# Third block of a three-block layer chain: rates and token tiles in one stage, rates on 128 rows, the last two levels of the chunk inverse on their own blocks, constant products between the first steps

## What is computed

```python
def gated_delta_rule(q, k, v, beta, g):
    q = l2_norm(q) * (dk ** -0.5); k = l2_norm(k)
...
    gc = jnp.cumsum(g, axis=-1)
    decay = jnp.exp(jnp.where(tril, gc[..., :, None] - gc[..., None, :], NEG_INF))
    kb = k * beta[..., None]; vb = v * beta[..., None]
    lmat = jnp.where(strict, jnp.einsum('bhncd,bhnsd->bhncs', kb, k) * decay, 0.0)
    rhs = jnp.concatenate([vb, kb * jnp.exp(gc)[..., None]], axis=-1)
    sol = lax.linalg.triangular_solve(lmat + eye, rhs, left_side=True, lower=True, unit_diagonal=True)
    value, k_cumdecay = sol[..., :dv], sol[..., dv:]
    attn_intra = jnp.einsum('bhncd,bhnsd->bhncs', q, k) * decay
    q_dec = q * jnp.exp(gc)[..., None]
    k_tail = k * jnp.exp(gc[..., -1:] - gc)[..., None]
    chunk_decay = jnp.exp(gc[..., -1])
...
```

## Time and profile before

| | |
|---|---|
| median of 3 runs | 2967.48 us (2950.17 to 2970.95) |
| profiled execution | 2967.56 us, span 2966.3 us |
| instructions | 42485 |
| PE busy | 2829.5 us, 95% of the span |
| PEld / DVE / ACT / POOL busy | 2379.1 / 1608.9 / 1058.5 / 614.5 us |
| mean granted clock of TensorE | 0.963 |
| DMA | 210.62 MB, mean 71 GB/s |

### The profile page before, as it was taken

One profiled execution on the slowest core, in us unless ns is written; L12 is line 12 of the kernel. 1 busy time (PEld: TensorE's weight loads), 2 busy tenths in 40 slices (PEclk: granted clock), 3 DMA queues, 4 the chain that ended last, 5 costly groups with the idle time before them and its releaser, 6 DMA issues. The chain is left out here.

```text
span 2966.3 us, 42485 instructions
## 1 busy us (share of the span) xinstructions
PE 2829.5 (95%) x16610; PEld 2379.1 (80%) x16610; DVE 1608.9 (54%) x2432; ACT 1058.5 (36%) x1793; POOL 614.5 (21%) x494
## 2 busy tenths in 40 slices
PE   8989999999999999998999999999898998999998
PEld 6768877778888766856788888976788898999986
DVE  5854556465553464944533336965344455576643
ACT  4362333432222323353423224545344233422223
POOL 2530101121100121441100003355355000111101
PEclk9987899999999999989999999998799999999999
DMA  4200132122223321302222222210000122222221
GB/s 155 94 1 7 65 107 71 36 87 94 97 93 99 111 67 56 100 15 78 88 98 93 92 94 78 86 44 1 6 2 1 44 86 72 86 93 93 92 94 64
DMA packets 60307, 210.62 MB, mean 71 GB/s; under 512 B 7926, under 2 KB 8566, under 8 KB 59990
## 3 DMA queue, kind: packets, MB, share of 16 engines
q1 hardware_dynamic: 58934, 207.39, 21.1%
q10 hardware_dynamic: 1184, 0.59, 0.1%
HBM read 205.84 MB, written 2.10 MB: 70 GB/s over the span
## 5 line engine op out<-in xcount | busy, mean ns | idle before, releaser
L272 PE MATMUL ps<-normed_hi,slab_hi 128*128 128x264 f32 (+2 forms) x2568 | 869.6, 339 | 27.5 <-DVE normed_lo L576 13.1
L274 PE MATMUL ps<-normed_hi,slab_lo 128*128 128x264 f32 (+2 forms) x2568 | 853.5, 332 | 0.0
L273 PE MATMUL ps<-normed_lo,slab_hi 128*128 128x264 f32 (+2 forms) x2568 | 852.1, 332 | 0.0
L153 ACT ACTIVATE slab_hi<-ring 128x1024 fp32r<-128x1024 f32 x376 | 397.2, 1057 | 967.0 <-PE ps L274 954.6
L157 DVE TENSOR_TENSOR slab_lo<-ring,slab_hi 128x1024 fp32r<-128x1024 f32 x360 | 481.3, 1339 | 384.8 <-ACT slab_hi L153 384.4
L272 PEld LDWEIGHTS ps<-normed_hi,slab_hi 128*128 128x128 f32 x2568 | 487.2, 190 | 95.8 <-issue 34.9
L273 PEld LDWEIGHTS ps<-normed_lo,slab_hi 128*128 128x128 f32 x2568 | 487.5, 190 | 52.1 <-issue 4.3
L274 PEld LDWEIGHTS ps<-normed_hi,slab_lo 128*128 128x128 f32 x2568 | 485.7, 189 | 48.9
L272 PE MATMUL ps<-hidden_hi,slab_hi 128*128 128x512 f32 x560 | 220.7, 394 | 5.6 <-DVE hidden_lo L223 5.6
L274 PE MATMUL ps<-hidden_hi,slab_lo 128*128 128x512 f32 x560 | 223.2, 399 | 0.0
L273 PE MATMUL ps<-hidden_lo,slab_hi 128*128 128x512 f32 x560 | 221.3, 395 | 0.0
(11 more groups left out here) (573 smaller groups left out, 4040.3 us busy)
## 6 DMA issues: line engine op xcount, KB each, us to landing
ring<-in_stream SPq DMA_DIRECT2D x376, 512.0 KB, 3.3
h<-in_x SPq DMA_DIRECT2D x8, 256.0 KB, 5.5
mix_y<-in_sgu_b SPq DMA_DIRECT2D x1, 1024.0 KB
out_features<-ffn_hidden SPq DMA_DIRECT2D x2, 512.0 KB, 3.2
xn<-in_c_recip_count SPq DMA_DIRECT2D x1, 512.0 KB, 3.3
rwkv_a<-in_mem SPq DMA_DIRECT2D x1, 512.0 KB, 3.9
rwkv_b<-in_mem SPq DMA_DIRECT2D x1, 512.0 KB, 5.0
sgu_ln<-in_sgu_ln SPq DMA_DIRECT2D x1, 512.0 KB
```

What stands on the lines that cost most here:

```text
L153: self.nc.scalar.activation(self.hi[:, n % PARTS, :], self.ring[:, n % SLOTS, :], ACT.Copy).then_inc(self.hi_ready, 1)
L272: nc.tensor.matmul(to, lhsT[0], rhs[0], start=start, stop=False)
L273: nc.tensor.matmul(to, lhsT[0], rhs[1], start=False, stop=False)
L274: return nc.tensor.matmul(to, lhsT[1], rhs[0], start=False, stop=stop)
```

## The change

The token turns move into the rates stage. There PE turns the rates, four of the 16 lots (v first), the sums of the chunks' ends, and then alternates 8 spreads with the 12 lots that are left. A spread now covers two heads at once, with a weight matrix `pair_pick` (128x512 in all) that ACT fills, and contracts over 128 rows. For this `heads` becomes `wide_heads` with 128 rows, of which POOL clears rows 2 and 3 during `mix_in_3_stage`, and ACT waits for that before it writes the heads. The stage's two dummy products are gone. In the chunk stage the levels with n = 32 and 64 run only on the rows `up` (0 to n) and the columns `down` (n to at most 2n), `alone` puts four dummy products of 128 columns on PE ahead of each of the steps 1 to 7, the sums contract over 128 rows, and DVE clears two more tiles.

```diff
-def gdn_rates_stage(K, heads, q, q0, tok, last_decay, zeroed):
+def gdn_rates_stage(K, wide_heads, q, q0, tok, last_decay, k_wide, zeroed, keys, values):
...
                 last.then_inc(turned, 1)
-                warm(K, 7, 2)
+                for n in range(FIRST):
+                    turn(n)
                 pe.wait_ge(last_in, 1)
                 for h in range(GDN_HEADS):
-                    last = nc.tensor.matmul(K.ps[:, 3, h * NC3:(h + 1) * NC3], K.pick(h, P), last_sum[:], start=True, stop=True)
+                    last = nc.tensor.matmul(K.ps[:, 1, h * NC3:(h + 1) * NC3], K.pick(h, P, P), last_sum[:], start=True, stop=True)
                 last.then_inc(spread, 1)
...
+                pe.wait_ge(picked, 1)
+                at = FIRST
+                for n in range(SPREADS):
+                    i, (lo, hi) = n // 2, HALVES[n % 2]
+                    if n >= 2:
+                        pe.wait_ge(q_out, n - 1)
+                    nc.tensor.matmul(K.ps[:, 2 + n % 2, 0:hi - lo], pair[:, i, :], wide_heads[:, 3, lo:hi], start=True, stop=True).then_inc(q_filled, 1)
+                    for _ in range(2 if n % 2 else 1):
+                        turn(at)
+                        at += 1
...
+        def sides(l):
+            if l < LV - 2:
+                return slice(0, C3), slice(0, C3), wide_prod
+            n = 32 << l - (LV - 2)
+            return slice(0, n), slice(n, min(2 * n, C3)), block_prod[l - (LV - 2)]
...
-                        last = nc.tensor.matmul(bank(q, 0)[:, i, :], wide_amask[:, q, i, :], wide_invT[:, q, i, :], start=True, stop=True)
+                        last = nc.tensor.matmul(bank(q, 0)[up, i, 0:width(down)], wide_amask[:, q, i, up], wide_invT[:, q, i, down], start=True, stop=True)
...
-                        last = nc.tensor.matmul(bank(q, 1)[:, i, :], wide_inv[:, q, i, :], wide_prod[:, q, i, :], start=True, stop=True)
+                        last = nc.tensor.matmul(bank(q, 1)[up, i, 0:width(down)], wide_inv[:, q, i, up], part[:, q, i, :], start=True, stop=True)
...
-                run(pairs=pairs, turn=turn, product=product, add=add, result=result)
+                run(alone=lambda: warm(K, 7, 4, P), pairs=pairs, turn=turn, product=product, add=add, result=result)
...
-                    nc.vector.tensor_tensor(invT[:, q], bank(q, 1), invT[:, q], ALU.add).then_inc(d_added[q], 1)
+                    at = invT[up, q, :, down]
+                    nc.vector.tensor_tensor(at, bank(q, 1)[up, :, 0:width(down)], at, ALU.add).then_inc(d_added[q], 1)
...
+                for t in block_prod:
+                    nc.vector.memset(t[:], 0.0).then_inc(padded, 1)
...
-            gdn_rates_stage(K, heads, gin[:, 0:4, 3:3 + T3], q0, tok, last_decay, (wide_k, attnT))
-            token_tiles_stage(K, [(gin[:, b + t, 3:3 + T3], (lambda c, n, to=to, t=t: to[:, c:c + n, t * P:(t + 1) * P]))
-                                  for b, to in ((4, k_tok), (8, v_tok)) for t in range(4)], C3, NC3)
+            gdn_rates_stage(K, wide_heads, gin[:, 0:4, 3:3 + T3], q0, tok, last_decay, wide_k, (attnT,),
+                            gin[:, 4:8, 3:3 + T3], (gin[:, 8:12, 3:3 + T3], v_tok))
```

More of the change, by code:

```diff
@@ L3016, in decays, with mix_in_3_stage @@
         nc.scalar.activation(heads[:, 1, :], heads[:, 1, :], ACT.Sigmoid)
-def mix_in_3_stage(K, network, fq, fk, fv, gin, heads, keep, causal, scale, factor, ins):
+def mix_in_3_stage(K, network, fq, fk, fv, gin, wide_heads, keep, causal, scale, factor, ins):
     nc = K.nc
@@ L3377, in _, with take @@
             @block.scalar
             def _(act):
+                heads_of = pair[:].rearrange("p i (o x) -> p (i o) x", x=HD)
+                nc.scalar.activation(heads_of, K.ident[:, 0:8].unsqueeze(2).to_broadcast((P, 8, HD)), ACT.Copy).then_inc(picked, 1)
+                def take(n):
+                    _, to, _, count, key = lots[n]
+                    act.wait_ge(tiles_turned, n + 1)
+                    if key:
+                        act.wait_ge(cleared, 1)
+                    nc.scalar.activation(to, tile(n)[:, 0:count * P].rearrange("p (i c) -> p i c", c=P), ACT.Copy).then_inc(tiles_out, 1)
@@ L3379, in _ @@
+                for n in range(len(lots)):
+                    take(n)
                 act.wait_ge(turned_out, 1)
@@ L3422, in own, with bank, width @@
             return t[0:C3, c, q:GDN_HEADS:2, :]
-        def bank(q, b):
-            return K.ps[0:C3, 4 * q + b, 0:QUAD * C3].rearrange("p (h i) -> p h i", i=C3)
+        def bank(q, b, rows=C3, columns=C3):
+            return K.ps[0:rows, 4 * q + b, 0:QUAD * C3].rearrange("p (h i) -> p h i", i=C3)[:, :, 0:columns]
+        def sides(l):
[3 more added lines that the diff above has]
+            return slice(0, n), slice(n, min(2 * n, C3)), block_prod[l - (LV - 2)]
+        def width(x):
+            return x.stop - x.start
         def head(base, h, c):
@@ L3438, in gdn_chunk_stage, with run @@
         APART = STEPS // 2 - 1
-        def run(**step):
+        def run(alone=None, **step):
             for n in range(NC3 * STEPS + APART):
+                if alone and 0 < n <= APART:
+                    alone()
                 for q in range(2):
@@ L3483, in product @@
                 def product(c, q, l, n):
+                    up, down, _ = sides(l)
                     if l == 0:
```

80 lines of the change are left out of this document (49 added, 31 removed).

## The result

| | before | after |
|---|---|---|
| median | 2967.58 us (18 runs, 2950.17 to 2970.95) | 2944.78 us (18 runs, 2928.15 to 2949.41) |
| ratio | | 0.9925, 95% interval 0.9915 to 0.9935 |
| profiled execution | 2967.56 us | 2928.15 us |
| rates and tokens, from the first rate turn to the chunk stage | 29.70 us | 18.68 us |
| chunk stage, to the scan's first product | 214.83 us | 205.27 us |

What follows compares the result with a forecast made beforehand. PE's half-speed work was taken to bound the rates stage; with both halves running, PE and the chain nearly tie. 12 + 6.5 + 6.3 - 2 = 22.8 us off 2967.56 gives 2944.8 us, range 2933 to 2957.

Steps and rivals of the forecast that it cites:

- Rates and tokens: Merged rates and token stage: 29.7 us falls to 17.5, saving 12 us, between 6.5 and 14.5.
- near 0.8: Sign in the new profile: the merged stage 17 to 18 us long with PE's mean granted clock near 0.8.
- turns do not lift the clock: Rival, merged stage: turns and 6-column sums keep PE at 1.2 GHz to its end; saving 6.6, 2950 us; chance 0.10.
- POOL's clearing: POOL's extra clearing of 128x1056 lies in a 17.4 us wait and costs nothing; without that cover about 1 us.
- The first chunk: Chunk stage's first chunk: constants hold 2.4 GHz; 3.8 + 4.1 - 0.8 - 0.6 = 6.5 us saved, between 7.5 and a loss of 3.
- The narrow levels: Levels n = 32 and 64 in the chunk stage: 1.7 + 2.8 + 1.8 = 6.3 us saved, from about 2 to some 12.
- 0.28 + 0.56 = 0.84: Narrow levels' saving: 0.28 us with half 0 narrow, six times; 0.56 with half 1 narrow, five times.
- 0.09 us for a change: Narrow levels on PE: each change of shape class costs about 0.09 us, five per narrow level, both together 0.9 us.
- 1.8 us forecast: End of the last chunk, half 1 alone: levels of 3.15 us become 2.1 and about 2.4, saving 1.8 us for both.
- narrow levels drop the clock: Rival, most chunks: each low-clock stretch costs up to 1.5 us, eight more make 2957 us; chance 0.07.
- Clock within the chunks: Chunk stage: two more stretches at 1.2 GHz than before charged, -2 us, between +3 and -12.

Runs made afterwards that it cites:

- e3: Changed kernel with rates and tokens again in two stages, as in the kernel before: 2956.56 us, ratio 0.9965 to the kernel before.
- e6: Changed kernel with narrow levels narrow only in moving columns, weights and transposes kept at 88 columns: 2951.30 us, ratio 0.9939 to the kernel before.
- e2: Changed kernel with all six levels on all rows and columns, without clearing the two narrow tiles: 2945.62 us, ratio 0.9917 to the kernel before.
- e8: Kernel before with the narrow levels alone (and POOL's clearing): 2962.43 us, ratio 0.9980 to the kernel before.
- e9: Kernel before with only the chunk-start sums contracted over 128 rows (and POOL's clearing): 2960.92 us, ratio 0.9977 to the kernel before.
- e4: Changed kernel with the chunk-start sums contracted over 8 rows, as before: 2948.03 us, ratio 0.9941 to the kernel before.
- e1: Changed kernel without the constant dummy products between the chunk stage's first steps: 2947.42 us, ratio 0.9941 to the kernel before.
- c2: Changed kernel with one product for chunk-end sums, tail constants, narrow tiles cleared on POOL, and two constants instead of four ahead of first steps: 2937.61 us.
- c3: Changed kernel with all levels full and one 48-column product for the chunk-end sums: 2942.14 us, ratio 0.9921 to the kernel before.
- c1: Changed kernel with one product for chunk-end sums, two constants ahead of the last seven steps, narrow tiles cleared on POOL: 2939.06 us, ratio 0.9909.

## Why the prediction came out as it did

The sum, 22.8 us off, is what the medians show (2967.58 - 2944.78 = 22.8). That it came out to the microsecond is luck: its parts missed in both directions. By place, the profiles show 11.0 us in the merged stage, 6.0 in the first chunk with the clearings, 3.5 in the four middle periods and nothing in the last chunk, 20.6 in all; the medians show 2 us more, which no stage explains.

**Rates and tokens: 12 us, measured 11.0** (29.70 to 18.68), 11.8 by the medians of e3. The structure was right, and the step that was off is the clock: 3.4 us at 1.2 GHz were charged beyond the rate turns and the first twelve token turns (3.7 us), and the stage ran 12.0 us at 1.2 GHz. The mean granted clock is 0.68, not near 0.8. That the sums might not lift the clock stood in the prediction; they did not, and took 3.3 us, inside the bounds of 1.9 and 3.9. The stage is 1.2 us longer than the 17.5 forecast, and 0.2 to 0.3 longer in e6 and e2, which have the same stage. The rival that turns do not lift the clock did not occur in full: the clock rose at 2053.5. In the merged stage no run separates the turns from the spreads beside them. But in all four profiles with a token stage of its own (the kernel before, e3, e8, e9) the clock rises 3.6 to 5.0 us into that stage, behind nothing but turns. For these turns the rule of the Trainium skill's page "TensorE: Matmul & The Clock Gate", Part 4, that full clock does not engage for transposes, does not hold.

**POOL's clearing: nothing, and so it was.** It takes 0.98 us, and the wait behind it shrank from 17.40 us to 16.29:

```profile
1795.46 0.98 POOL L3226 MEMSET head_rates<- 128x1056 f32 x1
1812.73 1.87 POOL L719 TENSOR_TENSOR norm_total<-xn 128x512 f32<-128x512 f32 x1 [16.29 <-ACT xn L711]
```

**The first chunk: 6.5 us, measured 6.0.** Half 0's pairs of the first two chunks stood 37.16 us apart and now 30.61, and the clearings on DVE cost the 0.6 us charged. The cause named is right, and by itself enough: with constants and 8-row sums (e4) the chunk takes 30.84 us. It is not the only one: with 128-row sums and no constants (e1, e9) it takes 34.07 and 33.52, half of the gain, which the prediction did not see. The constants stick out as forecast: a level with two groups of them is 3.41 us against 3.15, 0.13 us a group, and c2 with half of them wins 0.65 us over the seven groups. The clock was not at 1.00 throughout, as forecast, but at 0.94 in this execution.

**The narrow levels: 6.3 us, measured nothing (e2), 3.1 us where the clock is held (c3 against c1).** Two steps failed. The saving per period was taken as 0.28 + 0.56 = 0.84 and is 0.36. PE's busy time in a period fell by 0.8 us (28.15 to 27.32), but little of it comes through. With half 1 narrow its two levels and the wait for the result fall from 6.55 to 6.21 us; with half 0 narrow nothing comes through, 16.23 against 16.25 us from half 1's pairs to half 0's next. The timeline of PE there, in the changed kernel (half 0 at n = 32, then 64) and in e2:

```profile
2147.20 0.83 PE L3552 MATMUL ps<-gdn_invT,gdn_A_level 128*88 128x88 f32 x8
...
2150.05 0.51 PE L3548 MATMUL ps<-square_constants,gdn_invT 88*88 88x88 f32 x4 [0.24 <-DVE gdn_invT L3616]
2150.39 0.79 PE L3552 MATMUL ps<-gdn_invT,gdn_A_level 128*88 128x88 f32 x8
...
2153.50 0.51 PE L3548 MATMUL ps<-square_constants,gdn_invT 88*88 88x88 f32 x4
2153.84 0.79 PE L3552 MATMUL ps<-gdn_invT,gdn_A_level 128*88 128x88 f32 x8
```

```profile
2165.99 0.83 PE L3552 MATMUL ps<-gdn_invT,gdn_A_level 128*88 128x88 f32 x8
...
2169.34 0.79 PE L3552 MATMUL ps<-gdn_invT,gdn_A_level 128*88 128x88 f32 x8
...
2172.64 0.79 PE L3552 MATMUL ps<-gdn_invT,gdn_A_level 128*88 128x88 f32 x8
```

At n = 32 a level of both halves takes 3.19 us against 3.35, and PE waits 0.24 us for the chain of the other half. At n = 64 it takes 3.45 us against 3.30, longer than with full levels, and PE hardly waits: its changes of shape hold it. The prediction charged 0.09 us for a change. It had read that from two groups of which the second carries part of the cost too; the record spacing shows up to 0.16 (e4). Five of them take away more than PE saves at n = 64. At the end the levels are worth 1.6 of the 1.8 us forecast, and 2.2 to 2.5 are lost again, since the clock fell in them. The rival *narrow levels drop the clock* named the mechanism for most chunks; it struck in one place, the end, where half 1 is alone and no full products of the other half stand between.

**Clock within the chunks: -2 us.** In the middle chunks it was a gain of 0.85 us (two low stretches before, one after), at the end the loss of 2.2. About right as a sum, wrong in place.

**What the sum did not hold:** the 128-row sums. The prediction used them only as something that gives PE more to do. They save a change of shape, 0.31 us in each period (e4, e9), and alone bring 6.6 us in the median.

## What to carry to other kernels

When a product gets smaller, ask three things before counting its time: whether its weight columns shrink too (moving columns alone gave nothing here), whether it now differs in shape from its neighbours, and whether the engine still has enough to do there to keep its clock, above all where one chain runs alone. Replace many products with few columns by one product on a diagonal operand, and give neighbouring products one shape, even if that means contracting over 128 rows of which 8 carry data. And in an account of several edits, take back each one by itself: here the sum was right to a microsecond while its terms were wrong by up to six.

## What the hardware showed unexpectedly

- Eight products of 6 moving columns with 128 weight columns (16 records) took 3.3 us at 1.2 GHz, one product of 48 columns 0.3 us, and the clock rose 4.6 to 6.8 us after the stage's start instead of 10.0 to 12.0.
- Inside a group the records start 0.078 us apart with 8, 64 and 128 contraction rows alike, but a change of shape between two groups costs up to 0.16 us: two changes more in a period made it 0.31 us longer.
- With 88 weight columns the records start 0.078 us apart whether 24 or 88 columns move; with 64 weight columns 0.058, with 32 0.031.
- Adding four to eight short dummy records in a step made a lone chain faster (46.6 to 44.5 us), and two products of 128 columns held the clock as well as four.
- One early stretch takes 64 or 48 us for the same instructions, with 44 or 7 us of it at 1.2 GHz. These 16 us are more than any single part of this change brings.
